# Four more gate tiles as Strassen pairs, and fewer filling matmuls in the first block's attention

## The chip, the cores and the metric

The kernel runs on one NeuronCore of a Trainium2 chip. The metric is device time in microseconds (us) of one execution.

## The reference

Two transformer-like blocks on 1024 tokens of width 1024, all in fp32. The first block, cut to what matters here:

```
u  = rmsnorm(h) ; z = u @ w_in                      # q, k, v (12 heads of 64), pz, ga, gp
a  = dilated window attention(q, k, v)              # three head groups, dilation 1, 4, 16, 128 + 128 keys
p  = pooling branch(pz)
h  = h + (sigmoid(ga) * (a @ w_att_out) + sigmoid(gp) * (p @ w_pool_out)) @ w_out
h  = h + relu(rmsnorm(h) @ w_mlp_in)^2 @ w_mlp_out
```

The gates ga and gp are 1024 wide each: 16 tiles of 128 channels. The second block has a neighbourhood attention, a recurrent branch, two gates and an MLP of the same size.

## The kernel before

**Products.** Channels lie on partitions, tokens along the free axis. Each fp32 product is done as three fp32r matmuls of 128x512 (high x high, high x low, low x high), so every weight tile is first split into a high part (a copy on ACT) and a low part (a subtraction on DVE). A "unit" is one weight tile of 128 output channels over all 1024 tokens: 8 x 2 x 3 = 48 matmuls into one pair of banks, ps. `wstream` holds the units, and `split_hi` and `split_lo` split them.

**Strassen pairs.** q, k, v and the pooling input z (24 tiles) are made two tiles at a time by `projections`: seven products of 12 matmuls each instead of eight, 84 matmuls a pair. P_UNITS lists the tiles. ACT copies the banks (`proj_copy`), DVE adds and scales (`proj_out_tile`, `proj_scale`), and SP stores the result to DRAM (`proj_store`). The attention loads it from there.

**Start and attention of block 1.** Four gate units come first (N_START), then 12 Strassen pairs, then the attention. The attention has 6 head pairs of 8 steps, numbered s = 0 to 47, plus four closing steps. q below is the step within a head pair. A step treats two 128-query tiles. For group 0 they have 256 keys (but for the first), for group 1 alternately 128 and 256, for group 2 only 128. On TensorE (`double_step`): the scores of steps s and s+1 are made together in every even step, followed by the values of two earlier steps; then in each step come the transposes of the probabilities of step s-2 (`transpose_pair`) and some matmuls of a gate unit as filling (`fill`), whose number `fill_of` gives: 12 a step up to s = 39, 8 up to 47, then 2. In two steps of each head pair but the last (q = 5 and 6, for the fifth pair q = 4 and 5) a batch of the next pair's values is transposed first (`v_batch`), then half of the filling runs, then the transposes, then the other half.

DVE does for each step two additions of the distance bias and two maxima (`add_max`), then whatever is due: `gate_out` (one step after a unit is done), the low part of q or k of the next pair (`first_operand_lo`, q = 5 and 6), `split_lo` (two steps after), `pooled` and `pool_lo`. ACT does `v_out` (copy of the transposed values, when a batch was made), `probs_pair`, `o_out` in every fourth step, two `exp`, then what is due: `pool_hi`, `first_operand_hi` (q = 4 and 5), `unit_hi` (one step after a unit), `gate_tanh` (three steps after). Each engine takes its own list in order.

Three waits tie them. The scores of an even step wait until DVE has added all tiles of the step before (s_add). The additions of step s wait for the transposes of that step (s_T), which free their buffer. The transposes of a batch step wait for `v_out` (s_vev), since both use bank pa[:, 2]. Which steps get which of the extra pieces follows from `fill_of` through `unit_at`.

**Block 2's first Strassen pair.** `second_attention` of ACT and DVE prepares the operands T1, T3, T2 and T4 (sums of halves of the activation, 128x2048) and the first pair's weights between other work: `cover_out` evicts the units that run ahead, `second_t_sum`, `second_t_hi`, `second_t_lo` make the T operands, `proj_hi` and `proj_lo` the weights, `proj_copy` frees banks. TensorE's products come in the order B11, T1, B21, B22, T3, T2, T4.

Of the kernel before, what the change touches and what calls it, by code (L numbers as in the profile page):

```python
# [123 lines left out]
U_MIX, U_AO, T_MIX, T_AO = (16, 17), (24, 25), 16, 28  # L124
U_PO = [18 + n if n < 6 else 20 + n for n in range(KT)]
T_PO = [22 + n if n < 6 else 30 + n for n in range(KT)]
T_END = {U_MIX[0]: 19, U_MIX[1]: 22, U_AO[0]: 32, U_AO[1]: 36}
# [4 lines left out]
def build(nc, xT, wstream, wproj, wff1, wff2, vecs, consts, mask2, bias2, outT, x2, hres, hff, proj, gates):  # L132
    ctx = ExitStack()
    with ctx:
# [386 lines left out]
        def _(sp):  # L521
# [148 lines left out]
            def proj_store(i):  # L670

                for o in range(2):
# [3 lines left out]
                    sp.dma_start(proj[2 * i + o], proj_out(i)[:, o]).then_inc(sem(f"s_hst{i % 2}"), 16)  # L676
# [110 lines left out]
            load_unit(sp, 19, 1)  # L787
# [4 lines left out]
            for u in range(20, 23):  # L792
# [3186 lines left out]
```

## Time and profile before

| | |
|---|---|
| median of 3 runs | 2764.09 us (2763.79 to 2764.26) |
| the profiled execution, its own time | 2763.09 us |
| its span in the profile | 2761.3 us |
| TensorE (PE) busy | 2745.4 us, 99% of the span, 13154 matmuls |
| DVE, ACT, POOL busy | 1926.1, 1381.7 and 109.5 us |
| granted TensorE clock, mean | 0.999 |
| Strassen pairs of block 1 | 55.68 to 284.16 us of the span |
| attention of block 1 | 284.16 to 484.46 us |
| Strassen pairs of block 2 | from 1353.79 us |

Busy time of PE counts a matmul from its start to its modelled end, and ends overlap the next start. So a time per matmul is best read from one start to the next.

### The profile page before, as it was taken

What the parts mean: (1) busy time and instruction counts of PE and PEld (TensorE: products, weight loads), DVE (VectorE), ACT (ScalarE), POOL (GpSimd) and SP (SyncE); (2) the same over time, 40 slices, a digit from 0 to 9 for tenths busy, and PEclk for the clock granted to TensorE, in tenths of its full rate; (3) what the DMA queues carried; (4) which work ended last, traced back from release to release, by engine and by line L of the source; (5) the groups of instructions that cost most, each with busy time, mean ns of one, the idle gap of its engine ahead of it and who ended that gap; (6) DMA issues with size and microseconds to landing.
All of it is one profiled execution on the core that took longest, in us unless ns stands there. A gap on an engine that the chain in (4) does not pass through costs nothing.

```text
span 2761.3 us, 35045 instructions
## 1 busy us (share of the span) xinstructions
PE 2745.4 (99%) x13154; PEld 2243.5 (81%) x13154; DVE 1926.1 (70%) x2768; ACT 1381.7 (50%) x2218; POOL 109.5 (4%) x106
## 2 busy tenths in 40 slices
PE   9999999999999999999999999999999999999998
PEld 8888877788888888888787778888888888888887
DVE  8877556766866667688946653888546866666786
ACT  7332566424655544454446551888424555554452
POOL 0000112000000000000003320000000000000000
PEclk9999999999999999999999999999999999999999
DMA  4333433423344385541352121212223344384442
GB/s 162 118 110 114 162 108 108 153 99 140 146 155 154 133 318 174 158 129 58 137 178 62 54 77 46 61 54 61 77 82 140 141 153 152 138 327 159 158 134 73
DMA packets 103158, 356.32 MB, mean 129 GB/s; under 512 B 11216, under 2 KB 11344, under 8 KB 96848
## 3 DMA queue, kind: packets, MB, share of 16 engines
q1 hardware_dynamic: 101696, 349.37, 36.3%
q10 hardware_dynamic: 1296, 4.72, 0.5%
q8 instruction: 106, 1.74, 0.3%
q14 instruction: 60, 0.49, 0.1%
HBM read 251.28 MB, written 102.76 MB: 128 GB/s over the span
## 4 chain that ended last, share of the span: by engine, by line
PE 80%; DVE 2%; issue 1%; ACT 0%; POOLq 0%; POOL 0%; DVEq 0%; ACTq 0%
PE ps L506 17%; PE pa L3650 11%; PE ps L3650 11%; PE ps L3679 9%; PE pa L3679 9%; PE ps L3258 6%; PE pa L506 4%; PE ps L3697 3%; PE ps L3565 2%; PE ps L3295 1%; PE pa L3386 1%; PE pa L3431 1%; PE pa L3397 1%; PE pa L3295 1%; PE ps L3548 0%
## 5 line engine op out<-in xcount | busy, mean ns | idle before, releaser
L1749 ACT ACTIVATE krh<-k_rraw 128x512 fp32r<-128x512 f32 x192 | 121.1, 631 | 230.4 <-PE ps L3679 115.8
L2775 DVE TENSOR_TENSOR krl<-k_rraw,krh 128x512 fp32r<-128x512 f32 x192 | 132.6, 690 | 132.2 <-ACT krh L1749 132.1
L496 DVE TENSOR_TENSOR w_lo<-w_raw,w_hi 128x1024 fp32r<-128x1024 f32 (+1 forms) x100 | 118.0, 1180 | 141.0 <-ACT w_hi L490 140.9
L490 ACT ACTIVATE w_hi<-w_raw 128x1024 fp32r<-128x1024 f32 (+1 forms) x100 | 101.7, 1018 | 196.8 <-PE ps L506 112.2
L506 PE MATMUL ps<-a_hi,w_hi 128*128 128x512 f32 x576 | 177.5, 389 | 0.0
L506 PE MATMUL ps<-a_hi,w_lo 128*128 128x512 f32 x576 | 177.3, 389 | 0.0
L506 PE MATMUL ps<-a_lo,w_hi 128*128 128x512 f32 x576 | 177.3, 389 | 0.0
L3650 PE MATMUL pa<-xh,fwh 128*128 128x512 f32 x448 | 174.5, 389 | 0.0
L3650 PE MATMUL ps<-xh,fwh 128*128 128x512 f32 x448 | 174.3, 389 | 0.0
L3650 PE MATMUL ps<-xh,fwl 128*128 128x512 f32 x448 | 174.3, 389 | 0.0
L3650 PE MATMUL pa<-xh,fwl 128*128 128x512 f32 x448 | 174.3, 389 | 0.0
L3650 PE MATMUL ps<-xl,fwh 128*128 128x512 f32 x448 | 174.3, 389 | 0.0
L3650 PE MATMUL pa<-xl,fwh 128*128 128x512 f32 x448 | 174.3, 389 | 0.0
L3258 PE MATMUL ps<-a_hi,w_hi 128*128 128x512 f32 x480 | 160.4, 410 | 0.2 <-ACT res L1139 0.2
L3258 PE MATMUL ps<-a_lo,w_hi 128*128 128x512 f32 x480 | 155.8, 400 | 0.1
L3258 PE MATMUL ps<-a_hi,w_lo 128*128 128x512 f32 x480 | 154.5, 398 | 0.0
L3679 PE MATMUL ps<-krh,klh 128*128 128x512 f32 x384 | 150.2, 391 | 0.0
L3679 PE MATMUL ps<-krh,kll 128*128 128x512 f32 x384 | 149.4, 389 | 0.0
L3679 PE MATMUL ps<-krl,klh 128*128 128x512 f32 x384 | 149.4, 389 | 0.0
L3679 PE MATMUL pa<-krh,klh 128*128 128x512 f32 x384 | 149.4, 389 | 0.0
L3679 PE MATMUL pa<-krl,klh 128*128 128x512 f32 x384 | 149.4, 389 | 0.0
L3679 PE MATMUL pa<-krh,kll 128*128 128x512 f32 x384 | 149.4, 389 | 0.0
(468 smaller groups left out, 6780.8 us busy)
## 6 DMA issues: line engine op xcount, KB each, us to landing
k_rraw<-hff SPq DMA_DIRECT2D x224, 256.0 KB, 2.8
w_raw<-wstream SPq DMA_DIRECT2D x100, 512.0 KB, 3.6
hff<-hbuf SPq DMA_DIRECT2D x32, 1024.0 KB, 3.8
wA<-wff SPq DMA_DIRECT2D x16, 2048.0 KB, 7.8
hff<-hbuf SPq DMA_DIRECT2D x32, 768.0 KB, 3.2
w_raw<-wff SPq DMA_DIRECT2D x32, 512.0 KB, 4.3
f_raw<-wff SPq DMA_DIRECT2D x32, 512.0 KB, 4.4
proj<-res SPq DMA_DIRECT2D x24, 512.0 KB, 6.1
```

What stands on the lines that cost most here:

```text
L490: nc.scalar.activation(w_hi[:, slot, 0:n], w_raw[:, slot, 0:n], ACT.Copy).then_inc(s_whi, 1)
L496: nc.vector.tensor_tensor(w_lo[:, slot, 0:n], w_raw[:, slot, 0:n], w_hi[:, slot, 0:n].bitcast(F32), ALU.subtract).then_inc(s_wlo, 1)
L506: mm = nc.tensor.matmul(out[0:m, c], w[0:kp, slot, wofs:wofs + m], x[0:kp, k, c * HC:(c + 1) * HC], start=first and n == 0, stop=last and ...
L1749: nc.scalar.activation(k_r[e % 4][0][:], k_rraw[:, r % 4], ACT.Copy).then_inc(sem("s_khi"), 1)
L2775: nc.vector.tensor_tensor(k_r[e % 4][1][:], k_rraw[:, r % 4], k_r[e % 4][0][:].bitcast(F32), ALU.subtract).then_inc(sem("s_klo"), 1)
L3258: mm = nc.tensor.matmul(pair(t)[:, c], w[:, u % 2, k * P:(k + 1) * P], x[:, k, c * HC:(c + 1) * HC], start=(k == 0 and n == 0), stop=(k == ...
L3295: mm = nc.tensor.matmul(out, w[:, k * P:(k + 1) * P], x, start=n not in (2, 3, 6) and k == 0 and j == 0, stop=k == 3 and j == 2, skip_grou ...
L3386: mm = nc.tensor.matmul(out, lhsT, rhs, start=n == 0, stop=n == 2)
L3565: mm = nc.tensor.matmul(pair(t)[:, c], w[:, u % 2, P * k:P * k + P], x[:, half(c)], start=k == 0 and n == 0, stop=k == NPOOL - 1 and n == 2)
L3650: mm = nc.tensor.matmul(out, w[:, k * P:(k + 1) * P], x[:, k], start=n not in (2, 3, 6) and k == 0 and j == 0, stop=k == 3 and j == 2, ski ...
L3679: mm = nc.tensor.matmul(bank(y, n), w[:, n * P:(n + 1) * P], x[:], start=fresh and k == 0 and j == 0, stop=k == NKT - 1 and j == 2, skip_g ...
L3697: mm = nc.tensor.matmul(bank(0, n), w[:, kk], x[:, k], start=False, stop=hf == 1 and kk == 7 and w is wl, skip_group_check=True)
```

## The change

Four of the sixteen gate tiles of block 1 (a6, a7, p6, p7) leave the unit stream and become two more Strassen pairs, the fifth and the sixth of now 14. Their tanh is done on ACT inside `projections` (`pair_tanh`), and SP stores them behind the other gates in DRAM. The attention has 8 gate units as filling instead of 12, and `fill_of` gives 7 matmuls a step, then 6. The SP queue of the attention is written anew: one unit load and one gate store for each head pair, and the loads of q, k and v two pairs ahead behind them. In block 2 the preparation of T4 is moved behind that of the B21, B22 weights on DVE, and behind `cover_out(3)`, four weight copies and two bank copies on ACT; the bank copy for product 6 of the first pair is moved from n = 4 to n = 0. The rest renumbers.

```diff
-GATES = ([("p", n) for n in range(6)] + [("a", n) for n in range(8)] + [("p", n) for n in (6, 7)])
+GATES = [("p", n) for n in range(6)] + [("a", n) for n in range(6)]
+PAIR_GATES = [("a", 6), ("a", 7), ("p", 6), ("p", 7)]
 P_UNITS = [("v", 0), ("q", 0), ("k", 0), ("v", 1), ("q", 1), ("k", 1), ("z", 0), ("z", 1),
+           ("ga", 6), ("ga", 7), ("gp", 6), ("gp", 7),
...
@@ def proj_store(i)
-                    sp.dma_start(proj[2 * i + o], proj_out(i)[:, o]).then_inc(sem(f"s_hst{i % 2}"), 16)
+                    dst = proj[2 * i + o]
+                    if i in GATE_PAIRS:
+                        sp.wait_ge(sem("s_ptanh"), 2 * (i - GATE_PAIRS[0]) + o + 1)
+                        dst = gates[N_GATE + 2 * (i - GATE_PAIRS[0]) + o]
+                    sp.dma_start(dst, proj_out(i)[:, o]).then_inc(sem(f"s_hst{i % 2}"), 16)
...
             for k in range(N_PAIR1):
-                if k:
-                    if k + 1 < N_PAIR1:
-                        v_load(k + 1)
-                        qk_load(k + 1)
-                    if k == 4:
-                        z_load(4)
-                        z_load(5)
-                    gate_store(2 * k + 3)
-                if k + 1 < N_PAIR1:
-                    load_unit(sp, 2 * k + 8, 0)
-                gate_store(2 * k + 4)
-                if k + 1 < N_PAIR1:
-                    load_unit(sp, 2 * k + 9, 1)
-            load_unit(sp, 18, 0)
-            gate_store(N_GATE - 1)
+                load_unit(sp, 8 + k, k % 2)
+                gate_store(4 + k)
+                if k + 2 < N_PAIR1:
+                    v_load(k + 2)
+                    qk_load(k + 2)
+                if k == 3:
+                    z_load(4)
+                    z_load(5)
+            load_unit(sp, U_PO[0], 0)
+            for m in (N_GATE - 2, N_GATE - 1):
+                gate_store(m)
...
@@ def fill_of(b, s)
-            return 12 if s < 40 else 8 if s < 48 else 2
+            return 7 if s < 48 else 6
...
+            def pair_tanh(i, o):
+
+                if o == 0:
+                    act.wait_ge(sem("s_pj11"), i + 1)
+                act.wait_ge(sem("s_pjsc"), 3 * i + 2 * o + 1)
+                x = proj_out(i)[:, o]
+                nc.scalar.activation(x, x, ACT.Tanh, scale=0.5).then_inc(sem("s_ptanh"), 1)
...
@@ ACT, projections
                         proj_hi(i + 1, n)
+                        if i - 1 in GATE_PAIRS and n in (2, 3):
+                            pair_tanh(i - 1, n - 2)
...
@@ ACT, second_attention
                 proj_hi(0, 0, 2)
                 proj_hi(0, 1, 2)
-                second_t_hi(T4)
                 cover_out(3)
                 proj_hi(0, 2, 2)
                 proj_hi(0, 3, 2)
                 proj_copy(0, 0, 0, 2)
                 proj_hi(0, 4, 2)
                 proj_copy(0, 1, 1, 2)
+                second_t_hi(T4)
                 proj_hi(0, 5, 2)
                 proj_hi(0, 6, 2)
                 for i in range(LASTP2):
                     for n in range(7):
-                        if n == 4 or i and n < 2:
+                        if i and n in (0, 1, 4):
                             proj_copy(i, n, n, 2)
                         proj_hi(i + 1, n, 2)
+                        if i == 0 and n == 0:
+                            proj_copy(i, 4, 4, 2)
...
@@ DVE, second_attention
                 proj_lo(0, 0, 2)
                 proj_lo(0, 1, 2)
+                proj_sum(0, 1, 2)
                 second_low()
-                second_t_sum(T4)
-                proj_sum(0, 1, 2)
                 proj_lo(0, 2, 2)
                 proj_lo(0, 3, 2)
+                second_t_sum(T4)
                 second_t_lo(T3)
```

## Rows read from the trace of the kernel before

**Rows 1.** Windows: stretch, length, busy time (count) by engine, clock, DMA.
```profile
55.68:284.16 228.48, 228.48 (x1009) 189.25 (x1008) 177.14 (x271) 74.83 (x123) 0.11 (x1) 1.00 0.37 122
284.16:484.46 200.30, 198.73 (x1334) 156.83 (x1332) 118.06 (x252) 125.68 (x303) 37.62 (x30) 1.00 0.33 114
```

**Rows 2.** Timeline of PE, steps 4 and 5: start, us, instruction, count, idle before.
```profile
306.57 0.70 PE L3258 MATMUL ps<-a_hi,w_hi 128*128 128x512 f32 x2
...
309.40 0.60 PE L3359 MATMUL pa<-cst,qkv 128*128 128x128 f32 x4
309.76 0.71 PE L3258 MATMUL ps<-a_hi,w_hi 128*128 128x512 f32 x2
...
311.52 0.63 PE L3409 MATMUL pa<-cst,sm 128*128 128x128 f32 x4
```

**Rows 3.** Timeline of ACT, the end of step 4 and v_out of step 5.
```profile
308.90 1.04 ACT L1157 ACTIVATE qk1h<-qkv 128x1024 fp32r<-128x1024 f32 x1
...
310.80 0.58 ACT L1218 ACTIVATE vtok<-pa 128x512 f32<-128x512 f32 x1
```

**Rows 4.** Timeline of DVE, steps 14 and 15, 256 keys.
```profile
352.84 0.42 DVE L2324 SCALAR_TENSOR_TENSOR sm<-cst,pa 128x256 f32<-128x256 f32 x1 [2.94 <-PE pa L3409]
...
354.41 1.22 DVE L2112 TENSOR_TENSOR og<-ps,rb 128x1024 f32<-128x1024 f32 x1
355.54 1.22 DVE L2237 TENSOR_TENSOR qk1l<-qkv,qk1h 128x1024 fp32r<-128x1024 f32 x1
...
357.46 0.41 DVE L2324 SCALAR_TENSOR_TENSOR sm<-cst,pa 128x256 f32<-128x256 f32 x1
```

**Rows 5.** Timeline of PE, steps 14 to 16.
```profile
352.70 0.71 PE L3258 MATMUL ps<-a_hi,w_hi 128*128 128x512 f32 x2
...
357.46 0.79 PE L3386 MATMUL pa<-qk1h,qk1h 64*128 64x128 f32 x2
357.93 0.43 PE L3386 MATMUL pa<-qk1h,qk1l 64*128 64x128 f32 x2
```

**Rows 6.** Timeline of DVE, step 40, 128 keys.
```profile
459.25 0.29 DVE L2324 SCALAR_TENSOR_TENSOR sm<-cst,pa 128x128 f32<-128x128 f32 x1 [1.96 <-PE pa L3409]
...
460.30 0.17 DVE L2088 TENSOR_TENSOR first<-win,cst 128x16 f32<-128x16 f32 x1
...
461.89 0.28 DVE L2324 SCALAR_TENSOR_TENSOR sm<-cst,pa 128x128 f32<-128x128 f32 x1
```

**Rows 7.** Timeline of PE, steps 36 and 37, 128 keys.
```profile
443.75 0.70 PE L3258 MATMUL ps<-a_hi,w_hi 128*128 128x512 f32 x2
...
448.16 0.41 PE L3409 MATMUL pa<-cst,sm 128*128 128x128 f32 x2 [0.95 <-ACT vtok L1218]
```

**Rows 8.** Timeline of ACT, step 36, the first work after its exp.
```profile
445.55 1.05 ACT L1157 ACTIVATE qk1h<-qkv 128x1024 fp32r<-128x1024 f32 x1
```

**Rows 9.** Timeline of PE, block 2's first Strassen pair.
```profile
1359.00 0.39 PE L3295 MATMUL pa<-th,pwl 128*128 128x512 f32 x1
1361.52 0.47 PE L3295 MATMUL pa<-a_hi,pwh 128*128 128x512 f32 x1 [2.13 <-ACT p_p L1127]
...
1372.28 0.39 PE L3295 MATMUL pa<-th,pwl 128*128 128x512 f32 x1
1374.65 0.47 PE L3295 MATMUL pa<-th,p2wh 128*128 128x512 f32 x1 [1.98 <-DVE pwl L2179]
```

**Rows 10.** Timeline of ACT, the same stretch.
```profile
1356.94 1.92 ACT L1089 ACTIVATE th<-tr 128x2048 fp32r<-128x2048 f32 x1 [10.20 <-DVE tr L2132]
1358.76 1.09 ACT L1305 ACTIVATE c_stage<-ps,vec 128x1024 f32<-128x1024 f32 x1
...
1360.80 0.58 ACT L1127 ACTIVATE p_p<-pa 128x512 f32<-128x512 f32 x1
...
1373.96 0.59 ACT L1127 ACTIVATE res<-pa 128x512 f32<-128x512 f32 x1
```

**Rows 11.** Timeline of DVE, the same stretch.
```profile
1354.62 2.29 DVE L2132 TENSOR_TENSOR tr<-tr,tr 128x2048 f32<-128x2048 f32 x1
```

More of the change, by code:

```diff
@@ L122 @@
 N_UNITS = _u
[L124 to L127, printed above, removed]
+U_MIX, U_AO, T_MIX, T_AO = (N_GATE, N_GATE + 1), (N_GATE + 8, N_GATE + 9), N_GATE, N_GATE + 12
+U_PO = [N_GATE + (2 + n if n < 6 else 4 + n) for n in range(KT)]
+T_PO = [N_GATE + (6 + n if n < 6 else 14 + n) for n in range(KT)]
+T_END = {U_MIX[0]: N_GATE + 3, U_MIX[1]: N_GATE + 6, U_AO[0]: N_GATE + 16, U_AO[1]: N_GATE + 20}
 T_END.update({U_PO[n]: T_PO[n] + 1 for n in range(KT)})
@@ L357, in gate_at @@
                 return g_stage[m][:]
-            return og[:, 4 + m % 2] if m < 14 else g_stage[m - 10][:]
+            return og[:, 4 + m % 2] if m < OG_GATES else g_stage[m - OG_GATES + 4][:]
         def proj_raw(i, o, h):
@@ L394, in dilation @@
             kind, p = P_UNITS[j]
-            return 1 if kind == "z" else DIL[p // 2]
+            return DIL[p // 2] if kind in ("q", "k", "v") else 1
         def proj_half(i, o, c):
@@ L473, in build @@
         PLO_STEPS = {12: 0, 20: 1, 28: 2, 36: 3, 42: 4, 47: 5}
+        GATE_PAIRS = (4, 5)
         LASTP, LASTP2 = N_PROJ - 1, N_PROJ2 - 1
@@ L732, in gate_load @@
             def gate_load(kind, n, slot):
-                m = GATES.index((kind, n))
-                sp.wait_ge(sem(f"s_gst{m % 2}"), 16 * (m // 2 + 1))
+                if (kind, n) in PAIR_GATES:
+                    m = N_GATE + PAIR_GATES.index((kind, n))
+                    _, par, count = stored_of("g" + kind, n)
+                    sp.wait_ge(sem(f"s_hst{par}"), count)
+                else:
+                    m = GATES.index((kind, n))
+                    sp.wait_ge(sem(f"s_gst{m % 2}"), 16 * (m // 2 + 1))
                 sp.dma_start(gslot[:, slot], gates[m]).then_inc(sem(f"s_big{slot}"), 16)
@@ L786, in _ @@
                 gate_load("p", n, n)
-            load_unit(sp, 19, 1)
+            load_unit(sp, U_PO[1], 1)
             for n in range(3, 6):
@@ L791, in _ @@
                 gate_load("a", n, 6 + n)
-            for u in range(20, 23):
+            for u in U_PO[2:5]:
                 load_unit(sp, u, u % 2)
@@ L796, in _ @@
                 gate_load("a", j + 2, j)
-                load_unit(sp, 23 + j, (23 + j) % 2)
+                load_unit(sp, U_PO[5] + j, (U_PO[5] + j) % 2)
             for j in (4, 5):
@@ L800, in _ @@
                 gate_load("a", j + 2, j)
-            load_unit(sp, 27, 1)
+            load_unit(sp, U_PO[7], 1)
             for n in range(2):
@@ L804, in _ @@
                 gate_load("p", 6 + n, 6 + n)
-            for u in (28, 29):
+            for u in (STAGES["out1"].u, STAGES["out1"].u + 1):
                 load_unit(sp, u, u % 2)
@@ L846, in _ @@
             sp.wait_ge(sem("s_prod1"), 7 * (PB2 + LASTP2) + 1)
-            sp.wait_ge(sem("s_gst0"), 128 + 32)
+            sp.wait_ge(sem("s_gst0"), 8 * N_GATE + 32)
             sp.dma_start(v_in[0][:], proj[0]).then_inc(sem("s_ldq1"), 16)
@@ L850, in _ @@
             sp.dma_start(qk2[:, 0, 0], proj[1]).then_inc(sem("s_ldq0"), 16)
-            sp.wait_ge(sem("s_gst1"), 128 + 16)
+            sp.wait_ge(sem("s_gst1"), 8 * N_GATE + 16)
             sp.dma_start(qk2[:, 0, 1], proj[2]).then_inc(sem("s_ldq0"), 16)
@@ L1087, in second_t_hi @@
                 if o == T4:
-                    act.wait_ge(sem("s_gst0"), 128 + 32)
+                    act.wait_ge(sem("s_gst0"), 8 * N_GATE + 32)
                 nc.scalar.activation(t_op[o][0][:], t_raw[o][:], ACT.Copy).then_inc(sem("s_xh"), 1)
@@ L1100, in proj_hi @@
                     elif b == 2:
-                        act.wait_ge(*((sem("s_gst1"), 128 + 16), (sem("s_ldz1"), 64), (sem("s_fin"), KT))[n - 4])
+                        act.wait_ge(*((sem("s_gst1"), 8 * N_GATE + 16), (sem("s_ldz1"), 64), (sem("s_fin"), KT))[n - 4])
                     elif n == 6:
@@ L1240, in o_out @@
                     if c in (8, 10):
-                        act.wait_ge(sem("s_gst0" if c == 8 else "s_gst1"), 16 * 7)
+                        act.wait_ge(sem("s_gst0" if c == 8 else "s_gst1"), 8 * OG_GATES)
                     src = pa[:, 3]
@@ L2107, in gate_out @@
                     dve.wait_ge(sem("s_rb"), 1)
-                if 6 <= m < 14:
+                if 6 <= m < OG_GATES:
                     dve.wait_ge(sem(f"s_gst{m % 2}"), 16 * (m // 2))
-                elif m >= 14:
+                elif m >= OG_GATES:
                     dve.wait_ge(sem("s_S"), UNITS_PER_PAIR * 5)
@@ L3849, in projection_weights @@
 def projection_weights(w, w2):
-    first = {"v": 12, "q": 0, "k": 6, "z": 18}
+    first = {"v": 12, "q": 0, "k": 6, "z": 18, "ga": 24, "gp": 32}
     out = np.zeros((P, N_PROJ + N_PROJ2, 2, KT, P), np.float32)
@@ L3974 @@
     args.append(nc.dram_tensor("proj", (2 * N_PROJ, P, S), F32, kind="Internal").ap())
-    args.append(nc.dram_tensor("gates", (N_GATE, P, S), F32, kind="Internal").ap())
+    args.append(nc.dram_tensor("gates", (N_GATE + len(PAIR_GATES), P, S), F32, kind="Internal").ap())
     build(nc, *args)
```

1 line of the change is left out of this document (added).

## The prediction

> **What bounds the kernel now.** First the busy table: PE is busy 99% of the span, so time falls where PE gets fewer matmuls and grows where it idles. Then the windows of two stages [rows 1]: in block 1's Strassen pairs PE never idles, 1008 matmuls in 228.48 us, 0.2267 us each from start to start. In the attention DVE is busy 118.06 and ACT 125.68 of 200.30 us, neither the bound by its sum; but PE depends on them step by step, so I went on to timelines of steps. Last I looked for PE's gaps over the whole span: two of over 2 us stand in block 2's first Strassen pair [rows 9].
>
> **Removed work.** Four units are 4 x 48 = 192 matmuls, two pairs 2 x 84 = 168: 24 less, -5.44 us at 0.2267 [rows 1]. The pairs' stage grows by 2 x 19.04 us, the attention loses 43.5 us of filling. In the pairs' stage DVE has 177.14 and ACT 74.83 of 228.48 us [rows 1]. ACT gets two tanh of about 1 us more in a pair, behind `proj_hi` for products 2 and 3, each hidden by 12 matmuls, 2.72 us. On SP the gate pair's store waits for them, with a weight load behind it that has a whole pair of time. I take 0; without that cover four tanh would cost 4 us.
>
> **Block 2's first pair.** PE waits from 1359.00 to 1361.52 and from 1372.28 to 1374.65, less 0.2267 each 2.29 + 2.14 = 4.44 us [rows 9]. The first wait ends with a bank copy begun at 1360.80; ahead of it stand T4's high part, begun at 1356.94 after a DVE sum of 2.29 us, and `cover_out(3)` [rows 10, 11]. In the new order ACT evicts when its unit is done, about 1354.2: 1.1 us, two weight copies 1.1 us, then the bank copy, possible after product 0 (1353.79 + 2.72), ends about 1357.4, and PE wants it at 1359.23. T4's pieces come about 3 us later, and those of T3 and T2 queue with them: on DVE T3 and its weight are ready at 1362.6, T2 at 1365.6, T4 at 1368.6; PE wants them at 1364.67, 1367.39 and 1370.11, 1.5 to 2.1 us later. The second wait ends with the copy at 1373.96 [rows 10], which stood behind copies that wait for DVE's sums; ahead of them it can run at 1367.4. I take -4.44 us, between 0 (as much wait appears elsewhere) and -4.44.
>
> **Filling of 7 instead of 12.** T is the end of a step's transposes on PE, E the extra DVE work of that step.
>
> (a) `v_out`. 12 fillings take 309.40 - 306.57 = 2.83 us, so 7 take 1.70 and 3 take 0.79; the batch takes 0.36 [rows 2]. From T of q = 4 PE needs 2.85 us to its next transposes. ACT ends its exp 2.33 us after T (308.90), each extra piece takes (310.80 - 308.90)/2 = 0.95, and from the start of `v_out` to the transposes are 0.72 [rows 2, 3]. PE waits 3.05 + 0.95n - 2.85: 1.15 us with one extra piece, 2.10 with two. With 128 keys the exp end 1.80 us after T [rows 7, 8]: 0.62 and 1.57.
>
> (b) Scores of an even step behind DVE. DVE starts 0.14 us after T, needs 1.57 for two tiles, then E, then 1.20 to the end of the next step's second addition; PE goes on 0.06 later [rows 4, 5]: 2.97 + E. PE gets there in 1.70 + 0.35 (transposes) + 1.70 + 0.22 = 3.97 us, with 0.22 for the change to scores. It waits E - 1.00. A `gate_out`, `split_lo` or `first_operand_lo` takes 1.13 us [rows 4], `pooled` 1.6 [rows 6]. With 128 keys (1.05 and 0.81 [rows 6], transposes halved) it waits E - 1.73, in group 1 E - 1.52.
>
> (c) Batch steps: at q = 6 three fillings less stand behind T and (b) is 0.68 us longer; at q = 5 DVE needs 1.40 us against PE's 1.24, a wait of 0.16.
>
> With 12 fillings the same rules give the waits of now: 0.3 us at steps 5 and 13 (311.52 against 309.76 + 1.47 [rows 2]), 0.3 to 0.4 at 8 and 16 [rows 5], 1.1 at 37 [rows 7]; 2.4 in all.
>
> With 7, units are done after steps 3, 10, 17, 23, 30, 37, 44 and 51, which places the extras. By head pair:
> First: (a) with `first_operand_hi` and `unit_hi` 2.10, (c) 0.16 and, E = 1.13, 0.81: 3.07.
> Second: step 8 `pooled` 0.60, (a) with one 1.15, 0.16, 0.81: 2.72.
> Third: 0.08, (a) with two 1.57, 0.16, 0.29: 2.10.
> Fourth: step 24, `gate_out` and `pooled`, 1.21; 0.62, 0.16, 0.29: 2.28.
> Fifth: step 32, E = 2.73, 1.00; step 37 with only four fillings behind T 1.30; step 38, E = 2.26, 0.53: 2.83.
> Sixth: none.
> Sum 13.0 us, and 0.5 for step 14, where two ACT pieces meet: 13.5, less the 2.4 of now, +11.1 us. Bounds: 7 us of waits (only `v_out`'s, the others taken up) and 20 (half as much again, if late pieces push the next ones).
>
> The new SP queue costs nothing: a pair's q and k wait for scores six steps, about 17 us, before they are wanted (s = 30 and 36), and the stores and unit loads ahead of them are due by s = 26.
>
> **Total:** -5.44 - 4.44 + 11.1 = +1.2 us on the profiled execution's own 2763.09, 2764.3 us; the median of the runs is 1.0 us above it, so I predict 2765.3 us, within 0.2% (5.5 us), about what a measurement of this kernel can tell from no change.
>
> A rule speaks against short filling. PE's longest wait now is 2.3 us, the granted clock 1.00 [rows 1, 9], and none that I forecast is longer: by the rows the clock costs 0. The Trainium skill, page "TensorE: Matmul & The Clock Gate", section "HAM oscillation — how this bites in real kernels", says that recurring pauses of PE can put its clock back to half. By that rule the result would be rival 4.
>
> **The rivals.**
> 1. Faster: queues absorb the short filling, and PE keeps its present 2.4 us: -9.9 us, 2754.2. For it: both engines would be busy under 80% of the stage. Against: step 37, where even 6 fillings behind a batch don't cover `v_out` [rows 7]. It decides when all waits are under 6.8 us. Chance 0.12.
> 2. Slower: `v_out` becomes the pace of every batch. If each of the ten waits 2.10 us, 21 in place of 7.2, the total is +15, 2779; it decides from 17.8 us of waits in all, a mean of 1.2 a batch. For it: ACT's order puts `v_out` behind every late piece of the step before. Against: I find such a wait in six of ten. Chance 0.18.
> 3. Block 2's reordering only moves its wait: +4.4 on the forecast, 2769.8. T4 comes 3 us later with 1.5 in hand. Chance 0.08, half of it slower.
> 4. PE's clock falls in the attention: 0.23 us more for a filling (an estimate, 0.2267 doubled), 9 us if a tenth of the 384 is hit, 2774. Against: 1.00 in all rows. Chance 0.02.
> The forecast: 0.60.
>
> Faster by over 0.2%: 0.12. Slower: 0.18 + 0.04 + 0.02 = 0.24. The same: 0.64. The forecast's own range, waits of 9.5 to 17.5 us, is 2761.3 to 2769.3; the range for 8 in 10 reaches into rivals 1 and 2, 2757 to 2773.
>
> **What would show it.** The pairs' stage is 266.5 us without idle. The attention is about 168 us; without the waits it would be 154. Its waits end with `v_out` (transposes of q = 5) and with DVE's additions (scores of even steps), largest at steps 5 and 24; none is over 2.3 us. Block 2's first seven products follow each other at 2.72 us. I am wrong if the attention's waits are under 7 or over 18 us, or if a gap stands before T3, T2 or T4.

## The result and the profile after

| | before | after |
|---|---|---|
| median, compared on the same chip | 2764.18 us (20 runs) | 2769.15 us (20 runs, 2767.86 to 2771.95) |
| ratio to before | | 1.0018, 95% interval 1.0012 to 1.0024 |
| profiled execution, its own time and span | 2763.09, 2761.3 us | 2768.76, 2767.0 us |

The kernel is 4.97 us slower, 0.18%: inside the 0.2% that the prediction called the same, near its slow edge. The forecast was 2765.3 us, 1.2 above before.

First the page of the profile after. PE has 24 matmuls less than before (13130) and almost the same busy time; the span is 5.7 us longer.

```profile
span 2767.0 us, 35081 instructions
PE 2745.0 (99%) x13130; PEld 2241.3 (81%) x13130; DVE 1943.5 (70%) x2800; ACT 1388.2 (50%) x2234; POOL 109.7 (4%) x106
```

The windows of four stages after: block 1's pairs, its attention, block 2's pairs, and the down product of MLP 2. The columns are those of [rows 1]; length less PE's busy time is idle time.

```profile
core 0: us, PE busy (x) PEld busy (x) DVE busy (x) ACT busy (x) POOL busy (x), PEclk, DMA share, GB/s
56.25:322.81 266.56, 266.56 (x1177) 220.72 (x1176) 202.66 (x311) 90.39 (x147) 0.11 (x1) 1.00 0.35 121
322.81:492.98 170.17, 159.41 (x1142) 122.26 (x1141) 110.04 (x244) 117.03 (x295) 37.84 (x30) 1.00 0.32 109
1362.39:1438.55 76.16, 76.16 (x337) 62.90 (x335) 50.55 (x66) 38.53 (x62) 3.94 (x4) 1.00 0.48 168
2441.61:2758.50 316.89, 315.84 (x1413) 260.21 (x1411) 232.41 (x362) 142.00 (x235) 2.03 (x2) 1.00 0.47 156
```

And two stages of before that [rows 1] doesn't have:

```profile
1353.79:1434.60 80.81, 76.69 (x337) 62.72 (x335) 50.55 (x67) 38.58 (x62) 3.93 (x4) 1.00 0.45 157
2437.37:2752.76 315.39, 315.21 (x1413) 260.43 (x1411) 232.58 (x362) 142.35 (x235) 2.02 (x2) 1.00 0.47 157
```

| stage, us | before | after | change | forecast |
|---|---|---|---|---|
| start, up to the first pair | 55.68 | 56.25 | +0.57 | 0 |
| block 1's pairs | 228.48 | 266.56 | +38.08 | +38.1 |
| block 1's attention | 200.30 | 170.17 | -30.13 | -32.4 |
| block 2's pairs | 80.81 | 76.16 | -4.65 | -4.44 |
| MLP 2, down | 315.39 | 316.89 | +1.50 | 0 |
| all the rest | | | +0.3 | 0 |

The start lies between 55.5 and 56.3 us in all profiles with the same code there, so its 0.57 is scatter. What is left are three statements: the two Strassen stages came out as computed, the attention is 2.3 us longer than forecast, and 1.5 us are lost 2000 us later, in a stage whose code the change doesn't touch.

**The waits of the attention.** PE's timeline around step 5; the bracket is the idle time before a group and what ended it. It answers to [rows 2].

```profile
343.00 0.63 PE L3279 MATMUL ps<-a_hi,w_hi 128*128 128x512 f32 x2
345.58 0.63 PE L3430 MATMUL pa<-cst,sm 128*128 128x128 f32 x4 [1.95 <-ACT vtok L1237]
345.96 0.70 PE L3279 MATMUL ps<-a_lo,w_hi 128*128 128x512 f32 x2
```

ACT at the same time, against [rows 3]: exp, then the two pieces that are due (`first_operand_hi`, L1174, and `unit_hi`, L494), then `v_out` (L1237).

```profile
342.46 0.51 ACT L1243 ACTIVATE sm<-sm,negm 128x256 f32<-128x256 f32 x1 [0.18 <-DVE negm L2349]
...
342.96 1.04 ACT L1174 ACTIVATE qk1h<-qkv 128x1024 fp32r<-128x1024 f32 x1
343.91 1.04 ACT L494 ACTIVATE w_hi<-w_raw 128x1024 fp32r<-128x1024 f32 x1
344.86 0.58 ACT L1237 ACTIVATE vtok<-pa 128x512 f32<-128x512 f32 x1
```

The other kind, DVE with `gate_out` (L2133) and `pooled` (L2109 to L2111) ahead of the additions of step 25, and PE's scores of step 26 behind them. They answer to [rows 4, 5].

```profile
413.92 1.22 DVE L2133 TENSOR_TENSOR og<-ps,rb 128x1024 f32<-128x1024 f32 x1
...
415.45 1.27 DVE L2111 SCALAR_TENSOR_TENSOR zf<-win,cst,zf 128x1008 f32<-128x1008 f32 x1
416.64 0.41 DVE L2345 SCALAR_TENSOR_TENSOR sm<-cst,pa 128x256 f32<-128x256 f32 x1
...
417.42 0.41 DVE L2345 SCALAR_TENSOR_TENSOR sm<-cst,pa 128x256 f32<-128x256 f32 x1
```

```profile
415.93 0.63 PE L3279 MATMUL ps<-a_hi,w_hi 128*128 128x512 f32 x2
417.11 0.33 PE L3407 MATMUL pa<-qk1h,qk1h 64*128 64x128 f32 x1 [0.55 <-DVE sm L2345]
417.89 0.33 PE L3407 MATMUL pa<-qk1h,qk1h 64*128 64x128 f32 x1 [0.46 <-DVE sm L2345]
```

PE waits twice there, once for each tile's addition. Step by step, each wait is the time from one start to the next less the usual time of such a change (0.23 us from fillings to transposes, 0.32 to scores, 0.16 from the first tile's first score to the second's):

| wait of PE, us | forecast | after |
|---|---|---|
| transposes of steps 5, 13, 21, 29, 37 behind `v_out` | 2.10, 1.15, 1.57, 0.62, 1.30 | 2.11, 1.17, 1.58, 0.64, 1.32 |
| transposes of step 14 (two ACT pieces) | 0.5 | 0.44 |
| scores of steps 8 and 16 | 0.81, 0.81 | 0.72, 0.72 |
| scores of step 10 (`pooled`) | 0.60 | 0, but see below |
| scores of steps 24 and 32 | 0.29, 0.29 | 0.34, 0.33 |
| scores of steps 26, 34, 40 | 1.21, 1.00, 0.53 | 1.24, 0.84, 0.58 |
| scores of steps 6, 14, 22, 30 | 0.16 each | 0.13 each |
| transposes of four steps q = 7 or 4, behind `probs_pair` or exp | not seen | 0.25 each |
| values ahead of the closing steps, behind `o_out` | not seen | 0.81 |

The 0.16 us hide a cost. Where DVE isn't late, the first scores of the two tiles start together, and the step has no such 0.16 us. Where DVE's second addition is late, they start apart, and the step's scores take 0.16 to 0.17 us more than the table's wait. Step 10 is the plain case: by the table it waits 0, and from start to start its scores take 1.19 us in place of 1.02.

The last row of the table in the trace (PE, step 47 to 48):

```profile
484.12 0.63 PE L3279 MATMUL ps<-a_hi,w_lo 128*128 128x512 f32 x2
485.49 0.66 PE L3452 MATMUL pa<-pt,vtok 128*64 128x128 f32 x8 [0.74 <-ACT og L1270]
```

**Block 2's first pair.** ACT evicts the unit (L1324), splits weights and copies the bank of the first product at 1365.31; against [rows 10] the T4 copy of 1.91 us (L1098) now follows the second bank copy. PE passes all seven products with 0.2267 us from start to start; the gaps of [rows 9] are gone, as the window of 76.16 us without idle time shows.

```profile
1362.59 1.12 ACT L1324 ACTIVATE c_stage<-ps,vec 128x1024 f32<-128x1024 f32 x1 [7.25 <-PE ps L3279]
1363.60 0.62 ACT L1115 ACTIVATE pwh<-w_raw 128x512 fp32r<-128x512 f32 x1
...
1365.31 0.60 ACT L1136 ACTIVATE p_p<-pa 128x512 f32<-128x512 f32 x1 [0.56 <-PE pa L3316]
...
1368.52 1.91 ACT L1098 ACTIVATE th<-tr 128x2048 fp32r<-128x2048 f32 x1
```

**MLP 2's down product.** PE there takes one 128x512 product after the other from blocks `krh`, `krl` (high and low part of the activation) that ACT and DVE make of `k_rraw`, loaded by SP through four buffers of 256 KB. Near the end of the stage after, PE stands twice, 0.70 and 0.50 us more than a matmul's time; before has nothing there. Followed back, the lateness begins 23 us earlier, with one load: ACT after waits 1.37 us for the second of two `k_rraw` loads.

```profile
2673.41 0.63 ACT L1776 ACTIVATE r6h<-k_rraw 128x512 fp32r<-128x512 f32 x1 [1.84 <-DMA k_rraw<-hff]
2675.41 0.63 ACT L1770 ACTIVATE krh<-k_rraw 128x512 fp32r<-128x512 f32 x1 [1.37 <-DMA k_rraw<-hff]
```

The same pair of copies before, where the second load is waited for 0.20 us:

```profile
2668.76 0.63 ACT L1755 ACTIVATE r6h<-k_rraw 128x512 fp32r<-128x512 f32 x1 [1.21 <-DMA k_rraw<-hff]
2669.59 0.63 ACT L1749 ACTIVATE krh<-k_rraw 128x512 fp32r<-128x512 f32 x1 [0.20 <-DMA k_rraw<-hff]
```

From there on SP's issues, which wait for DVE to free a buffer, are 1.6 us later than before, counted from the stage's start, until the slack ahead of PE is used up. The DMA view of that microsecond names the company the late load had: one packet of queue q8, of 16384 bytes, 0.92 us long. After, it starts at 2672.85, in the middle of the load's packets:

```profile
DMA  6999898846664424400200000000000000000050
...
q1 hardware_dynamic: 74, 0.12, 32.3%
q8 instruction: 1, 0.02, 5.8%
```

Before, a packet of the same queue starts at 2665.92, when the load's packets are through:

```profile
DMA  0400900000000000000000000000000000000000
...
q8 instruction: 1, 0.02, 5.8%
q1 hardware_dynamic: 5, 0.00, 1.2%
```

(First row: busy tenths of 16 DMA engines in 40 slices of this one microsecond.) Before has late loads in this stage too: one lands at 201 us of the stage, 1.8 us later than in the profile of after, behind a packet of q8 that began at 197.7; the issues behind it come when they do in after. So a late load alone isn't a loss; this one was, as the issues behind it were late. Whether the packet is the cause was the question of the last three runs.

### The profile page after: what moved, and what is told of

Its sections match the earlier page's. It is cut to its first block, busy times and chain, and to the rows that moved or that the text cites. A ratio compares the mean times of both kernels' runs of the same rounds, so it can differ in the third digit from the quotient of the medians.

```text
span 2767.0 us, 35081 instructions
## 1 busy us (share of the span) xinstructions
PE 2745.0 (99%) x13130; PEld 2241.3 (81%) x13130; DVE 1943.5 (70%) x2800; ACT 1388.2 (50%) x2234; POOL 109.7 (4%) x106
## 3 DMA queue, kind: packets, MB, share of 16 engines
q8 instruction: 106, 1.74, 0.3%
## 4 chain that ended last, share of the span: by engine, by line
PE 79%; DVE 2%; issue 1%; DMA 1%; ACT 1%; SPq 0%; POOLq 0%; POOL 0%; DVEq 0%; ACTq 0%
PE ps L510 17%; PE pa L3671 11%; PE ps L3671 11%; PE ps L3700 9%; PE pa L3700 8%; PE ps L3279 6%; PE pa L510 4%; PE ps L3718 3%; PE ps L3586 2%; PE pa L3316 1%; PE ps L3316 1%; PE pa L3407 1%; PE pa L3452 1%; PE pa L3418 1%; DMA k_rraw<-hff 1%
## 5 line engine op out<-in xcount | busy, mean ns | idle before, releaser
L494 ACT ACTIVATE w_hi<-w_raw 128x1024 fp32r<-128x1024 f32 (+1 forms) x96 | 97.5, 1016 | 199.4 <-PE ps L510 112.2
L510 PE MATMUL ps<-a_hi,w_hi 128*128 128x512 f32 x576 | 177.5, 389 | 0.0
L510 PE MATMUL ps<-a_hi,w_lo 128*128 128x512 f32 x576 | 177.3, 389 | 0.0
L510 PE MATMUL ps<-a_lo,w_hi 128*128 128x512 f32 x576 | 177.3, 389 | 0.0
L3279 PE MATMUL ps<-a_hi,w_hi 128*128 128x512 f32 x416 | 139.0, 406 | 0.5 <-ACT res L1148 0.5
L3279 PE MATMUL ps<-a_lo,w_hi 128*128 128x512 f32 x416 | 138.8, 404 | 0.0
L3279 PE MATMUL ps<-a_hi,w_lo 128*128 128x512 f32 x416 | 137.5, 403 | 0.0
```

The lines of the kernel that those rows point to most:

```text
L494: nc.scalar.activation(w_hi[:, slot, 0:n], w_raw[:, slot, 0:n], ACT.Copy).then_inc(s_whi, 1)
L510: mm = nc.tensor.matmul(out[0:m, c], w[0:kp, slot, wofs:wofs + m], x[0:kp, k, c * HC:(c + 1) * HC], start=first and n == 0, stop=last and ...
L3279: mm = nc.tensor.matmul(pair(t)[:, c], w[:, u % 2, k * P:(k + 1) * P], x[:, k, c * HC:(c + 1) * HC], start=(k == 0 and n == 0), stop=(k == ...
```

## The experiments

The first four were run on one chip, beside before at 2763.89 us, the next four on a second (2763.76), the last three on a third (2763.69). Before is 0.3 to 0.5 us lower there than in the result's comparison, and differences to after carry this much. The table has all; stages are in us of the profiled execution. The last column ends with the start of the stage's last matmul, some 0.17 us ahead of the windows above.

| kernel | time, us | ratio to before | attention | block 2's pairs | MLP 2 down |
|---|---|---|---|---|---|
| before | 2764.18 | | 200.3 | 80.81 | 315.2 |
| after | 2769.15 | 1.0018 (1.0012 to 1.0024) | 170.2 | 76.16 | 316.7 |
| e1, block 2 alone | 2759.35 | 0.9983 (0.9974 to 0.9992) | 200.3 | 76.16 | 315.2 |
| e2, all but block 2 | 2774.4 | 1.0036 (1.0023 to 1.0050) | 170.2 | 81.54 | 316.8 |
| e3, `v_out` early | 2762.98 | 0.9997 (0.9988 to 1.0006) | 165.0 | 76.16 | 316.3 |
| e4, other fillings | 2765.35 | 1.0004 (0.9995 to 1.0013) | 166.6 | 76.16 | 316.5 |
| e5, both | 2762.95 | 0.9995 (0.9986 to 1.0004) | 165.8 | 76.16 | 316.4 |
| e6, before, `proj` larger | 2763.84 | 0.9999 (0.9990 to 1.0008) | 200.3 | 80.78 | 315.2 |
| e8, table of fillings | 2755.51 | 0.9972 (0.9961 to 0.9982) | 157.0 | 76.16 | 316.5 |
| e9, one more ACT piece | 2779.34 | 1.0057 (1.0043 to 1.0071) | 178.1 | 76.16 | 316.8 |
| e10, after, 24 PE instructions more | 2768.36 | 1.0016 (1.0007 to 1.0025) | 171.5 | 76.16 | 315.3 |
| e11, before, 24 fewer | 2765.31 | 1.0005 (0.9996 to 1.0015) | 200.3 | 80.81 | 316.5 |
| e12, e8 with 24 more | 2755.34 | 0.9969 (0.9957 to 0.9981) | 156.9 | 76.16 | 315.8 |

**e1 and e2: one part alone.** e1 is the kernel before with only block 2's reordering, e2 the changed kernel with block 2's old order. The edit of e1, on ACT and DVE:

```diff
                 proj_hi(0, 1, 2)
-                second_t_hi(T4)
                 cover_out(3)
...
                 proj_copy(0, 1, 1, 2)
+                second_t_hi(T4)
                 proj_hi(0, 5, 2)
...
-                        if n == 4 or i and n < 2:
+                        if i and n in (0, 1, 4):
                             proj_copy(i, n, n, 2)
                         proj_hi(i + 1, n, 2)
+                        if i == 0 and n == 0:
+                            proj_copy(i, 4, 4, 2)
...
                 proj_lo(0, 1, 2)
+                proj_sum(0, 1, 2)
                 second_low()
-                second_t_sum(T4)
-                proj_sum(0, 1, 2)
                 proj_lo(0, 2, 2)
                 proj_lo(0, 3, 2)
+                second_t_sum(T4)
                 second_t_lo(T3)
```

> The kernel before with the reordering of block 2's first Strassen pair alone. The theory says that this part takes away the two waits of PE there and brings no other: 4.4 us less than before, about 2759.7 us. Rival: the wait only moves to another product or to the start of block 2's attention, or the gain is given back later: no change, 2764. In the trace of the full change a wait of 0.3 us appears at the end of these pairs, so 4.1 is possible too.

> The changed kernel with block 2's old order: the gate pairs and the short filling alone. If the two parts add, it is 4.4 us slower than the full change and 8 to 9.5 us slower than before, about 2773. By the sum of the prediction it would be +5.7 us. Rival: the parts don't add, because something late in block 2 depends on how block 1 ended: then it differs from before by the same 5 us as the full change.

e1 is 4.54 us faster than before, e2 10.5 slower than before and 5.25 slower than after. The two parts add up within what the intervals allow (10.5 - 4.5 = 6.0 against 5.0), and rival 3 falls: the wait in block 2 was removed and not moved. e1's window of block 2's pairs has no idle time:

```profile
1355.75:1431.91 76.16, 76.16 (x337) 62.88 (x335) 50.26 (x65) 38.81 (x62) 3.92 (x4) 1.00 0.48 167
```

So the part in block 1 costs 9.5 to 10.5 us by itself; e2, at 10.5, is above its expectation's 8 to 9.5. With block 2's old order the granted clock fell to half behind the first wait there in two of the four profiles, e2 (a wait of 3.0 us) and e6 (2.3 us, as before, where it stayed at 1.00). In e6 it cost nothing: PE would have waited 2.1 us later on anyway, and the stage has 80.78 us against 80.81. e6's window behind that wait:

```profile
1362.00:1367.00 5.00, 5.00 (x17) 3.92 (x16) 5.00 (x4) 1.91 (x4) 0.00 (x0) 0.66 0.00 0
```

**e3: `v_out` ahead of the late pieces.** In the changed kernel ACT takes the `v_out` of the next step right behind the exp, ahead of whatever is due.

```diff
-                    if p + 1 < N_PAIR1 and V_STEP[1][p] <= q < V_STEP[1][p] + VB[1]:
-                        v_out(VB[1] * (p + 1) + q - V_STEP[1][p])
...
                             exp(2 * s + hh)
+                    pn, qn = divmod(s + 1, STEPS_PER_PAIR)
+                    if pn + 1 < N_PAIR1 and V_STEP[1][pn] <= qn < V_STEP[1][pn] + VB[1]:
+                        v_out(VB[1] * (pn + 1) + qn - V_STEP[1][pn])
```

> The changed kernel with ACT's copy of the transposed values taken right behind the exp of the step before, ahead of the extra pieces; nothing else moves. Theory: PE's waits at steps 5, 13, 21, 29 and 37 (6.8 us in the trace) fall to under 0.5 each, some 0.5 to 1 us comes back where probabilities are copied later: 5 to 6.5 us less than the full change, about 2763. Rival: DVE sets the pace of these steps as well, and PE waits as long at the next scores: no more than 1 us less, 2768.

6.2 us faster than after. PE around step 5, in e3:

```profile
342.37 0.63 PE L3280 MATMUL ps<-a_hi,w_hi 128*128 128x512 f32 x2
343.08 0.63 PE L3431 MATMUL pa<-cst,sm 128*128 128x128 f32 x4
343.47 0.70 PE L3280 MATMUL ps<-a_lo,w_hi 128*128 128x512 f32 x2
```

No bracket stands behind the transposes. The five waits of 6.8 us are 0.24, 0.24, 0.25, 0.25 and 0.38; one of 0.94 us came back at step 15, where the late pieces now stand ahead of `probs_pair`; the scores' waits stay. So the terms (a) are shown by their removal, which is worth 5.1 us in the attention (the median fell by 6.2).

**e4 and e5: where the fillings stand.** The same 384 fillings (24 ahead of the steps, 360 in them), but more of them in the two batch steps:

```diff
-            return 7 if s < 48 else 6
+            p, q = divmod(s, 8)
+            if s >= 48:
+                return 2
+            if p == 5:
+                return 8 if q < 6 else 7
+            return 11 if V_STEP[1][p] <= q < V_STEP[1][p] + 2 else 6
```

> The changed kernel with the same 360 fillings placed otherwise: 11 in the two batch steps of a head pair, 6 in the others, 8 or 7 in the sixth pair, 2 in the closing steps. Theory: in batch steps more filling hides ACT's copy (2.1, 1.2, 1.6, 0.6, 1.3 us of wait fall to about 2.0, 1.0, 0.5, 0.5, 0.5) and the scores of q = 6; the steps with 6 get some more wait behind DVE: 2 to 4 us less than the full change, 2765 to 2767. Rival: only the mean of the filling counts, 2769.

> Both single edits together: ACT's copy of the values taken early, and 11 fillings in batch steps, 6 elsewhere. They take away partly the same waits, so they shouldn't add (6.2 and 3.8 us would be 10): theory 6 to 8 us less than the full change, 2761 to 2763, with DVE's waits at steps 26, 34 and 40 (1.7, 1.3 and 1.0 us) as what is left. Rival: the two are independent, 2759.

e4 is 3.8 us faster than after: `v_out` costs 1.88, 0.94, 0.39, 0.40 and 0.40, but the scores of steps 26, 34 and 40, with one filling less ahead of them, 1.70, 1.30 and 1.27 instead of 1.24, 0.84 and 0.58. e5 takes both edits, and is no faster than e3. Its waits behind `v_out` are gone altogether and those of the scores are e4's. Against e4, step by step from start to start, 3.1 us went in two places to values, transposes and fillings that are slower by themselves, 1.55 in each. Its windows behind the waits of the scores of steps 34 and 40:

```profile
441.00:444.00 3.00, 3.00 (x12) 2.34 (x9) 1.05 (x4) 2.33 (x7) 2.92 (x2) 0.51 0.41 167
...
462.00:465.00 3.00, 3.00 (x10) 2.38 (x9) 2.58 (x7) 1.38 (x5) 0.00 (x0) 0.60 0.47 190
465.00:468.00 3.00, 3.00 (x25) 2.30 (x23) 1.05 (x4) 2.32 (x6) 2.81 (x3) 1.00 0.00 0
```

The granted clock is 0.51 and 0.60 for these three microseconds (the lower level, 1.2 GHz, for nearly all and for most of them) and 1.00 again behind. In PE's rows two fillings take 1.20 us from the first start to the last end, where they take 0.62 at full clock:

```profile
459.54 0.75 PE L3413 MATMUL pa<-qk1h,qk1h 64*128 64x128 f32 x2 [0.94 <-DVE sm L2351]
...
462.01 1.20 PE L3285 MATMUL ps<-a_lo,w_hi 128*128 128x512 f32 x2
...
463.87 0.87 PE L3285 MATMUL ps<-a_hi,w_hi 128*128 128x512 f32 x2
464.58 0.62 PE L3285 MATMUL ps<-a_lo,w_hi 128*128 128x512 f32 x2
```

That is rival 4's mechanism, and it appeared behind two waits of 1.3 us (0.95 to 1.0 for the first tile, 0.3 for the second), while the wait of 1.7 us at step 26 had full clock behind it. The profiled execution is the slowest of e5's eleven, so the others may have had less of it. But the mean clock of each timed execution is known too: the six slower ones of e5 (2762.95 to 2765.59 us) show 0.998, the five faster ones (2760.37 to 2762.47) 0.999, where e3 and e8 show 0.999 in all theirs. So the clock, by the profile and by these figures, took e5's gain over e3 from its median. The Trainium skill, page "TensorE: Matmul & The Clock Gate", section "HAM oscillation — how this bites in real kernels", says that recurring pauses of PE can put its clock back to half. The profile of the changed kernel shows none of it: 1.00 in the whole attention, with one wait of 2.1 us. In e5 the trace agrees.

**e9: the disputed wait made longer.** The changed kernel, with the high part of q made twice on ACT at q = 4, one piece more ahead of `v_out`:

```diff
+                        if q == OP_STEP:
...
+                            nc.scalar.activation(hi, score_operand(1, p + 1, 0)[0], ACT.Copy, scale=0.125
+                                                 ).then_inc(sem("s_dup"), 1)
+                            act.wait_ge(sem("s_dup"), p + 1)
```

> The changed kernel with the high part of q made twice by ACT in step q = 4 of each head pair (the same values), once more waited for: a dose of about 1.1 us of ACT ahead of the copy of the values. Theory: each of the five batch waits grows by this, 5.5 us more than the full change, 2774.5, and the others stay. Rival: if DVE or PE's own queue ended these waits, a piece more on ACT, busy under 70% of the stage, costs nothing, 2769.

10.2 us slower than after, about twice what the piece explains, and 4.8 above its expectation. The `v_out` waits are 3.21, 2.26, 2.68, 1.74 and 2.41: each grew by 1.10, 5.4 in all, so the rule for (a) holds with a third piece. The other part is the clock again, behind two of these waits. Its windows at the wait of step 5 and behind it (0.93 in the next 4 us):

```profile
342.00:346.00 4.00, 1.05 (x7) 0.57 (x5) 0.98 (x1) 3.92 (x6) 0.00 (x0) 1.00 0.00 0
346.00:350.00 4.00, 3.90 (x26) 2.97 (x28) 3.32 (x6) 2.75 (x6) 0.00 (x0) 0.65 0.02 4
```

The profiled attention grows by 7.9 us: 5.5 in the five waits, and 2.4 in the fillings, scores and values that run in the two stretches of lower clock, 1.2 in each. All other waits stay, as expected, but for the one at step 14, which lies in the second stretch and is gone there. The waits of 2.7 and 2.4 us at steps 21 and 37 had full clock behind them. This execution, 2777.38 us, is the fastest of e9's five; its mean clock is 0.998, and that of the slower ones 0.997 and three times 0.996. So the rest up to the median goes with more time at the lower clock, though no profile shows where.

**e8: every step its own number.** If the waits come from which pieces meet which step, a table of 52 fillings, each step as many as its pieces ask for, should remove them. e8 is e3 with such a table (its sum is 360 as before) and `split_lo` one step later:

```diff
+FILL1 = (3, 5, 5, 5, 7, 10, 11, 8, 7, 8, 4, 6, 9, 9, 12, 9, 5, 11, 4, 5, 6, 10, 9, 7, 5, 11,
+         5, 5, 4, 10, 14, 7, 6, 11, 2, 7, 11, 8, 7, 7, 9, 5, 6, 6, 5, 6, 11, 10, 2, 3, 1, 1)
-            return 7 if s < 48 else 6
+            return FILL1[s]
...
-                    if done_before(s, 2) is not None:
-                        m = done_before(s, 2)
+                    if done_before(s, 3) is not None:
+                        m = done_before(s, 3)
```

> The changed kernel with ACT's early copy, the split of unit weights on DVE one step later, and the 360 fillings set step by step, 1 to 14, more where ACT or DVE has extra pieces. Theory: if the waits come from the extra pieces meeting the short filling, as in rules (a) to (c), nearly all of them can be placed away: 10 to 14 us less than the full change, 2755 to 2759, that is 5 to 9 less than before. Rival: the stage has a floor given by the two engines' queues, and no order of fillings gets below the early copy with 11 and 6.

```profile
322.33:479.30 156.97, 156.01 (x1143) 121.54 (x1142) 110.88 (x244) 116.50 (x296) 38.86 (x30) 1.00 0.35 118
```

By the table's count some 1.5 us of waits are left in the attention (14.5 us in after, 2.5 in before), the clock is 1.00, and the kernel beats both: 13.6 us faster than after, 8.25 than before. The same matmuls, the same pieces on ACT and DVE: all of the 13 us was order, 6.2 of them the early `v_out` (e3), the rest the table together with the later `split_lo`, which no run takes apart.

**e6, e10, e11, e12: the 1.5 us in MLP 2.** All programs with 14 pairs have them, those with 12 (before, e1) don't. The first guess was the place of the data in DRAM: `proj` has four tiles more. e6 is the kernel before with that size:

```diff
-    args.append(nc.dram_tensor("proj", (2 * N_PROJ, P, S), F32, kind="Internal").ap())
+    args.append(nc.dram_tensor("proj", (2 * N_PROJ + 4, P, S), F32, kind="Internal").ap())
```

> The kernel before with the DRAM tensor proj four tiles longer and nothing else. All programs with the gate pairs show 1.1 to 1.6 us more in block 2's last MLP stage, at two waits of PE, where no instruction was changed; the kernel before and the one with block 2's part alone don't. If the place of the tensors in DRAM makes it, this run shows it too: 2765 and two waits of 0.5 to 0.7 us some 255 and 261 us after that stage begins. If not (the place of the program's code in its stream of instructions, for example), it is as before, 2764.

2763.84, and no such wait: not the place. Then the packet of q8. In all profiles those packets have 16384 bytes, and in that stage come 21 to 33 us apart, 27.3 on the mean, while PE takes a weight load and a matmul each 0.2267 us: 241 of them, and its waits besides. The change takes some 24 x 2 PE instructions away and moves waits, so the blocks of PE's instructions end elsewhere, and their loads fall at other times. (By how much wasn't derived: 48 instructions alone would be 5.4 us, and the packet came 2.7 later.) e10 adds six small matmuls (24 instructions) at PE's start to the changed kernel, e12 to e8; e11 takes six of the first matmuls on ones, which only keep PE spinning, from the kernel before.

```diff
             keep_busy(23)
+            for _ in range(6):
+                nc.tensor.matmul(pa[:, 0, P:P + 1], ones[:], ones[:, 0:1], start=True, stop=True)
```

> The changed kernel with six more matmuls of one column at TensorE's start (each two passes of a weight load and a matmul, 24 instructions in all). In every program with 14 pairs, MLP 2's down stage is 1.2 to 1.6 us longer than before: a packet of 16384 bytes of the instruction queue q8, 0.92 us long, runs at 231.1 to 231.6 us of the stage, in the middle of a k_rraw load's burst, and that load lands 1.4 us later than its fellows; in the programs with 12 pairs it runs at 228.6 to 228.8, just behind a burst. Theory (TensorE's instructions arrive in blocks, and the change moved where in the stage a block is loaded): the packet comes about 2.7 us earlier, at 228.7, no load is late, the stage takes 315.2 us again in place of 316.5, and the whole is 1.3 us shorter less the 1 to 2 us that the six matmuls add at the start: 2768.5 to 2770. Rival (the wait comes from the other data or from DVE's and ACT's order in that stage): the stage stays at 316.3 to 316.8 and the whole is 2770 to 2771.

> The kernel before with 17 in place of 23 of the first matmuls on ones (24 instructions of TensorE fewer; only that spinning at the start is left out, no part of the computation). The counterpart: by the theory of the instruction block the packet of q8 comes 2.7 us later, at 231.5 us of MLP 2's down stage, inside a load's burst, and the stage takes 316.3 to 316.8 in place of 315.2 us; the whole is 1.2 to 1.6 us longer than before, less up to 1 us if the first unit starts earlier: 2764.0 to 2765.5. Rival: the stage stays at 315.2 and the whole is 2763 to 2764.

> The kernel with the table of fillings and the early v_out (2755.5 us) with the same six matmuls at the start. By the theory of the instruction block its MLP 2 down stage is 315.2 in place of 316.5 us; less the 1 to 2 us at the start the whole is 2755 to 2757, the same within what can be measured, the stages 1.3 us shorter and 1 to 2 us longer. Rival: the stage stays at 316.5 and the whole is 2756.5 to 2757.5.

The window of the stage in e10:

```profile
2444.30:2759.80 315.50, 315.32 (x1413) 260.36 (x1411) 232.40 (x362) 142.17 (x235) 2.03 (x2) 1.00 0.47 157
```

and in e11:

```profile
2437.81:2754.50 316.69, 315.73 (x1413) 260.28 (x1411) 232.66 (x362) 142.27 (x235) 2.03 (x2) 1.00 0.47 156
```

Counted from the stage's start, the packet is at 228.6 us before and 231.2 after; in e10 at 228.7, and the waits are gone (idle 0.18 us in place of 1.05); in e11 at 231.1, and they are there (0.96 in place of 0.18), the late copy too:

```profile
2671.42 0.63 ACT L1749 ACTIVATE krh<-k_rraw 128x512 fp32r<-128x512 f32 x1 [1.36 <-DMA k_rraw<-hff]
```

24 instructions at 0.113 us are 2.7 us, the packet moved by 2.6 and 2.5. The load behind that copy lands 1.6 us later than before in after, 1.4 in e11 and 0.2 in e10. In e12 the packet comes at 228.8 and is still under way when the first packets of the next load begin at 229.5; half the loss stays (idle 0.46, a stage of 315.8 us), where 315.2 was expected. Unmade in the one kernel and made in the other, the cause is shown. The total times only agree with it: e11 is 1.6 us above before with an interval of 0.9996 to 1.0015; e10 and e12 pay their 1.1 to 1.7 us for the six matmuls at the start.

The Trainium skill bears on both halves of this. Page "Advanced Engine Details and Errata", section "ISA Cache", gives lines of 16 KB, 256 instructions; the trace agrees, with its packets of 16384 bytes every 241 loads and matmuls on the mean, waits not counted. Page "DMA: Bandwidth & Descriptors", section "Queues, rings and completion order", says that a DMA engine serves its queues in turn, a whole packet of one before the next; the trace fits this but doesn't show it, since its views don't name the engine of a packet: the 16384 bytes keep one of 16 engines 0.92 us, the 2 KB packets of the load mostly 0.08 and at most 0.7.

A loss of this kind needs no edit. In the profiles of e1 and e5 PE waits 1.2 and 0.8 us, for `kll`, at the same place in the down product of block 1's MLP (1256 and 1259 us of the span), before and after have nothing there, and e1 runs there what before runs. Whether a packet made these two was not tested.

One more came out of e10: its attention is 1.3 us longer than after's with the same code. The windows up to and behind the wait of 2.1 us at step 5 show why (the 1.3 us all lie in the fillings, scores and values behind it):

```profile
323.90:346.00 22.10, 20.82 (x133) 16.37 (x131) 13.61 (x25) 11.38 (x29) 3.33 (x3) 1.00 0.45 164
346.00:352.00 6.00, 5.33 (x39) 4.30 (x40) 3.85 (x6) 3.28 (x8) 0.00 (x0) 0.72 0.01 3
```

So the same wait was followed by full clock in after's profile and by half clock in this one.

## Why the prediction came out as it did

The forecast was right in sign and class, and 3.9 us too low: +1.2 us was forecast and +5.0 measured. Its own range, 2761.3 to 2769.3 us, held the time by 0.15 us. That was close to luck, since 1.5 us of the 3.9 came from a stage that the prediction didn't look at, and two errors inside the waits went against each other.

- **Removed work, block 1's pairs.** 266.56 us without idle time, as computed; two tanh more on ACT and one more store cost nothing.
- **Block 2's first pair.** -4.65 in the profile, -4.54 by e1, -4.44 forecast. T4, 3 us later, was in time. The 0.3 us in all other stages stay unexplained.
- **Term (a), `v_out`.** Right to 0.02 us at each of five places; e3 removed it, e9 made it longer by 1.10 us, where the rule has 0.95 a piece (this one is waited for by itself besides).
- **Term (b), scores behind DVE.** Steps 8, 16, 24, 26, 32, 34 and 40 within 0.16 us, as waits. Step 10 was counted by the rule for 256 keys, where the tiles of step 8, ahead of `pooled`, have 128 (DVE begins them 0.52 us apart, not 0.78), and had none.
- **The term that was mis-sized: "13.5, less the 2.4 of now, +11.1 us".** Summed from start to start by kind of change, from before to after: fillings -44.1, transposes after fillings +6.4, scores +6.7, values +0.8, the rest +0.1. The waits cost 13.9 us in place of 11.1; for the fillings the forecast had -43.5. Three pieces make up the 2.8: 0.9 in the transposes, mostly the four steps behind `probs_pair`, which the rules didn't have since they looked at ACT only in the batch steps; 0.8 before the closing values, behind `o_out`; and 1.2 in the scores. The last is two errors of opposite sign: the waits behind DVE rose by 4.8 us where 5.6 were forecast, most of that at step 10, and 1.9 us came from the 0.16 to 0.17 us by which the two tiles' first scores start apart wherever DVE's second addition is late. No rule had this.
- **A term that was missing: 1.5 us in MLP 2.** No rule looked there. It isn't a property of the edit but of where it puts the blocks of PE's instructions (e10, e11).
- **"None is over 2.3 us", "by the rows the clock costs 0".** True of the profiled execution. It isn't safe for the kernel: e10, whose attention is the same code, lost 1.3 us to the clock behind the 2.1 us wait. In the timed runs five of the changed kernel's twenty show a mean clock of 0.998, the others 0.999; one such fall moves the mean by only 0.0006 (e10's profile, with one, shows 0.999), so how often it happens stays open.

The sum with the measured terms is +38.1 - 44.1 + 13.9 + 0.1 - 4.65 + 1.5 + 0.3 = +5.1, against +4.97 by the medians; the spans of the two profiles differ by 5.7, which has the start's scatter of 0.57 in it. The rivals: 1 (queues absorb it) is false for a flat 7, and e8, with 6.9 a step on the mean unevenly placed and `v_out` early, brings the waits under the 6.8 us that it asked for; 2 is false, the batches differ as their pieces do; 3 is false (e1); 4 is false for the profile of after; its mechanism is there in e5, e9 and e10, at 1.2 to 1.55 us a fall where it put 9 us in all.

## What to carry to other kernels

When filling work is thinned, the waits aren't a matter of its sum but of each step's pieces: write down per step what each in-order engine owes, and give the step that many fillings; here that and the early copy were worth 13 us with the same work. Put a copy for which the next matmul waits ahead of everything that merely is due. And before explaining a loss in a stage that wasn't touched, look at the packets of the instruction queues there: 24 instructions at the start of a program moved 1.3 us in its last stage. Look, too, at the mean clock of every timed run and not of the profiled one alone: in e5 it separated the slower half from the faster.

## What the runs showed of the hardware

- A packet of 16384 bytes on an instruction queue, 0.92 us long, in the midst of a 256 KB load went with this load landing 1.4 to 1.6 us late (after, e11); behind the load it cost nothing (before, e10). It moved with the number of PE's instructions ahead of it, 2.6 us for 24.
- TensorE's clock went to its lower level, for 3 to 4 us, behind waits of 1.3 us (e5, twice), 2.1 (e10), 2.3 (e6, block 2; e9), 3.0 (e2, block 2) and 3.2 us (e9), and stayed at 1.00 behind waits of 1.7 (e5), 2.1 (after), 2.3 (before, block 2), 2.4 and 2.7 us (e9). The length of the wait alone doesn't decide it, and the same code had both, twice (after and e10, before and e6). What does was not separated here. In the attention a fall cost 1.2 to 1.55 us; ahead of another wait it cost nothing (e6).
